# Prompt attention of a hybrid decoder step: the query blocks of each head pair taken in the order 3, 0, 2, 1, 4, 5, 6, 7

## What is computed

```python
def query_block(c):
    t0 = c * Q_BLOCK
    pos_q = t0 + jnp.arange(Q_BLOCK)
    ...
    o_c, p_c = compressed_branch(qb, pos_q, kv_cmp, slopes)
    idx, valid = select_blocks(p_c, pos_q, n_sel)
    ...
    o_s = selected_branch(qb, pos_q, kv_g, idx, valid, slopes)
    ...
    o_w = window_branch(qb, pos_q, kv_wb, pos_k, slopes)
    return gate_branches(gb, o_c, o_s, o_w)
```

## Time and profile before

| | |
|---|---|
| time, median of 3 runs | 2187.79 us (2186.11 to 2189.29) |
| profiled execution, from its first to its last instruction | 2191.0 us |
| PE (TensorE matmul) busy | 2114.1 us, 96% |
| DVE (VectorE) busy | 1035.5 us, 47% |
| ACT (ScalarE) busy | 703.1 us, 32% |
| mean granted TensorE clock | 0.984 |
| prompt attention | 169.7 to 468 us of the span |

### The profile page before, as it was taken

One profiled execution on the slowest core, in us unless ns is written; L12 is line 12 of the kernel. 1 busy time (PEld: TensorE's weight loads), 2 busy tenths in 40 slices (PEclk: granted clock), 3 DMA queues, 4 the chain that ended last, 5 costly groups with the idle time before them and its releaser, 6 DMA issues.

```text
span 2191.0 us, 33624 instructions
## 1 busy us (share of the span) xinstructions
PE 2114.1 (96%) x14200; PEld 1827.4 (83%) x14200; DVE 1035.5 (47%) x1889; ACT 703.1 (32%) x1358; POOL 162.9 (7%) x164
## 2 busy tenths in 40 slices
PE   8999999989979999999999999999999999999997
PEld 7997777758639999999888886789888998889985
DVE  2136666636442466767221225644444344444447
ACT  3226677735431344444111112121111122111222
POOL 0021000001110122221000000000000000000007
PEclk9998999999999999999999999999999999999999
DMA  9322000135573222221321204121111111111101
GB/s 225 109 71 104 11 2 11 49 124 198 180 252 108 49 61 59 57 61 42 106 58 30 58 20 135 39 86 40 49 39 50 48 48 49 39 39 58 39 20 78
DMA packets 140626, 158.91 MB, mean 73 GB/s; under 512 B 25842, under 2 KB 122315, under 8 KB 135612
## 3 DMA queue, kind: packets, MB, share of 16 engines
q1 hardware_dynamic: 132444, 113.98, 17.3%
q0 software_dynamic: 8032, 42.78, 6.3%
HBM read 141.16 MB, written 19.76 MB: 73 GB/s over the span
## 4 chain that ended last, share of the span: by engine, by line
PE 89%; DMA 3%; DVE 3%; ACT 2%; issue 1%; SPq 0%; DVEq 0%; ACTq 0%; POOLq 0%
PE PS L834 62%; PE PS L1423 5%; PE PS L1056 3%; PE PS L1036 3%; PE PS L1139 3%; DMA arena<-in_cache_sel_kv,arena 2%; PE PS L1008 2%; PE PS L1010 1%; PE PS L1124 1%; PE PS L1349 1%; PE PS L1515 1%; PE PS L1065 1%; DMA arena<-in_x_prompt 1%; PE PS L1477 1%; PE PS L1292 1%
## 5 line engine op out<-in xcount | busy, mean ns | idle before, releaser
L834 PE MATMUL PS<-x_low,w_high_mlp 128*128 128x344 f32 x1056 | 338.1, 320 | 0.0
L834 PE MATMUL PS<-w_down_high,hidden 128*128 128x512 f32 x960 | 308.2, 395 | 0.9 <-DVE w_down_low L2547 0.9
L834 PE MATMUL PS<-x_high,w_low 128*128 128x344 f32 x768 | 246.1, 320 | 0.0
L2541 DVE TENSOR_TENSOR arena<-arena,PS 128x512 f32<-128x512 f32 x244 | 167.4, 687 | 134.9 <-PE PS L834 134.7
L834 PE MATMUL PS<-x_high,w_high_mlp 128*128 128x344 f32 x720 | 230.3, 320 | 0.0
L834 PEld LDWEIGHTS PS<-w_down_high,hidden 128*128 128x128 f32 x960 | 180.1, 188 | 54.3 <-DVE arena L2541 12.0
L834 PE MATMUL PS<-w_down_low,hidden 128*128 128x512 f32 x512 | 200.9, 392 | 0.0
L834 PEld LDWEIGHTS PS<-x_low,w_high_mlp 128*128 128x128 f32 x1056 | 198.6, 188 | 2.7
L834 PE MATMUL PS<-x_low,w_high_hgrn 128*128 128x344 f32 x600 | 192.6, 321 | 0.0
L834 PE MATMUL PS<-x_high_a,w_low 128*128 128x344 f32 x480 | 154.1, 321 | 0.0
L834 PE MATMUL PS<-x_high_b,w_low 128*128 128x344 f32 x468 | 149.7, 320 | 0.0
(11 more groups left out here) (390 smaller groups left out, 4285.0 us busy)
## 6 DMA issues: line engine op xcount, KB each, us to landing
wring<-in_w_in SPq DMA_DIRECT2D x100, 256.0 KB, 3.4
wring<-in_w_up SPq DMA_DIRECT2D x64, 256.0 KB, 3.2
arena<-in_w_down SPq DMA_DIRECT2D x16, 1024.0 KB, 5.0
arena<-in_x_prompt SPq DMA_DIRECT2D x16, 512.0 KB, 3.9
x_high_kept<-x_high_att SPq DMA_DIRECT2D x1, 4128.0 KB, 14.4
arena<-in_cache_win_kv SPq DMA_DIRECT2D x8, 512.0 KB, 4.5
arena<-in_w_out SPq DMA_DIRECT2D x2, 2048.0 KB, 8.8
out<-in_cache_win_kv SPq DMA_DIRECT2D x1, 4088.0 KB
```

Of the source, the lines that this page charges most:

```text
L834: mm = pe.matmul(out, w, x, start=(start and k == 0 and i == 0), stop=(stop and k == tiles - 1 and i == 2))
L2541: dve.tensor_tensor(y, y, PS[:, 5 + d % 3, :], ALU.add).then_inc(dn_dve, 1)
```

## The change

`job` looks the query block up in a table, so that every pair takes its blocks in the order 3, 0, 2, 1, 4, 5, 6, 7. Two functions that compute i for themselves (`out` and `factors`) use the same table. The PSUM bank that collects a block's output (6 or 7) went by the parity of i and now goes by the parity of the output number, which is the same bank in the old order. The fixed places j of `stage_k`, `low_k`, `stage_q` and `slope_row` stay.

```diff
+        ORDER = (3, 0, 2, 1, 4, 5, 6, 7)
+
         def job(j):
 
-            pair, i, wc, two = j // 32, j // 4 % NQ, j // 2 % 2, j % 2
+            pair, i, wc, two = j // 32, ORDER[j // 4 % NQ], j // 2 % 2, j % 2
             return 2 * pair + two, i, wc
...
-                        mm = pe.matmul(PS[HD * two:HD * (two + 1), 6 + i % 2, c:c + P], v[0:r, :],
+                        mm = pe.matmul(PS[HD * two:HD * (two + 1), 6 + n // 2 % 2, c:c + P], v[0:r, :],
...
-                pair, i = n // NQ, n % NQ
+                pair, i = n // NQ, ORDER[n % NQ]
                 act.wait_ge(ot_ps, 2 * n + 2)
-                act.activation(aT[:, pair, P * i:P * (i + 1)], PS[:, 6 + i % 2, 3 * P:4 * P], ACT.Copy).then_inc(o_act, 1)
+                act.activation(aT[:, pair, P * i:P * (i + 1)], PS[:, 6 + n % 2, 3 * P:4 * P], ACT.Copy).then_inc(o_act, 1)
...
-                pair, i = n // NQ, n % NQ
+                pair, i = n // NQ, ORDER[n % NQ]
                 dve.wait_ge(e_act, exps(4 * n + 3))
```

## The result

| | before | changed |
|---|---|---|
| time, median of 5 runs | 2189.29 us (2186.11 to 2191.27) | 2197.77 us (2194.99 to 2200.83) |
| ratio | | 1.0036, 95% interval 1.0023 to 1.0048 |
| profiled execution, span | 2191.0 us | 2194.0 us |
| mean granted clock in it | 0.984 | 0.984 |

The new order is slower, by 0.36% in these runs. The mean of all 17 is 2193.9 us; that of the 35 executions of the kernel before beside the twelve is 2189.1. So the loss is some 4 to 5 us, 0.2%, and the first five executions lay on its high side. Executions of one kernel lie several us apart (before: 2180.37 to 2194.51), and the granted clock explains most of it, as shown further down.

A forecast was written before the change was run, and what follows sets the result against it. TensorE was taken as the bound, with waits and low clock in each pair's first four blocks. Start +0.3, waits at changes of pair -1.5 and clock there +1.9 gave +0.7: 2188.5 us, range 2181.5 to 2195.5.

The forecast's parts named there:

- The waits at the start: First pair's start: TensorE dry 1.3 us before the first turn, then 2.6 us waiting for VectorE's copy at pv(1).
- The step that failed: First pair after pv(1): half clock until 189.1 us or 3.5 us more, four blocks ending at 205.8 against 205.5, +0.3 us.
- The changes of pair: Three changes between pairs: waits shrink or move, -0.5 us each, -1.5 us in all.
- Their clock: Clock at the three changes of pair: falls last half again as long beside narrower blocks, +1.9 us in all.
- The wait of 0.45 for the second copy of job 35: Change of pair: a new wait of pv(17), block 3's last product, for VectorE's copy, 0.45 us.
- the one behind the queries: Change of pair: TensorE's wait behind ScalarE's query preparation stays, 1.4 us where it was 1.50.
- the wait for block 7's sum: Change of pair: TensorE's wait of 0.47 us for the summed output would go.
- The slower one: Rival: clock stays down beside narrow blocks, middle 2194 us, chance 0.26; test: over 7 us at half from the second pair.
- the sum of the half-clock stretches: Sign over the attention: under 10 or over 38 us at half clock, against 24.0 before, would show the prediction wrong.
- the end of the first pair's fourth block: Sign at the start: the first pair's fourth block ends at 204 to 207 us.
- The faster one: Rival: 512-wide scores opening the attention and every pair keep the clock up, -6.4 us to 2181.4, chance 0.24.

The follow-up runs named there:

- e5: The changed kernel again, unaltered, for a second profile and twelve more executions: median 2190.80 us, ratio 1.0012.
- e14: The changed kernel unaltered, profiled a third time; no execution time given.
- e3: The new block order in the first pair alone, old order in the later pairs: 2193.79 us, ratio 1.0020 to the kernel before.
- e15: The kernel before, unaltered, profiled a second time; no execution time given.
- e4: Old order in the first pair, new order in the second to fourth: 2188.75 us, ratio 0.9996 to the kernel before.
- e9: e4 with the query preparation split by head into two halves, four jobs apart, on ScalarE and VectorE: 2186.58 us, ratio 0.9986.
- e10: The kernel before (old order) with the query preparation split by head into two halves: 2184.15 us, ratio 0.9974.
- e11: The kernel before (old order) with the first score product of jobs 0 to 11 issued three times: 2186.17 us, ratio 0.9993.
- e6: The changed kernel with VectorE's key preparation moved behind job 3's second-group copy, ScalarE's left at job 2: 2193.52 us, ratio 1.0017.
- e16: The same kernel as e6, profiled a second time: 2194.28 us for that execution.
- e1: The changed kernel with the second group's key preparation moved from job 2 to jobs 22 and 26, half at each: 2193.13 us, ratio 1.0014.
- e7: The changed kernel with the first pair in order 0, 3, 2, 1, 4, 5, 6, 7: 2188.80 us, ratio 1.0000 to the kernel before.
- e8: e3 with the first score product of jobs 4 to 15 issued three times: 2187.63 us, ratio 0.9996 to the kernel before.
- e2: The kernel before (old order) with the second group's key preparation moved from job 2 to jobs 22 and 26: 2191.77 us, ratio 1.0011.
- e13: Old order in all pairs, queries split by head, first score products of jobs 0 to 11 issued three times: 2181.04 us, ratio 0.9962.

## Why the prediction was wrong

**The waits at the start were about right.** TensorE dry ahead of the first turn: 1.3 us expected, 1.58 measured. pv(1) at 184.2 to 185.0: it started at 184.74, after a wait of 2.22 for VectorE's copy (2.6 expected). Idle time up to there: 5.6 us expected, 4.0 measured.

**The step that failed is the one behind it,** "If it is at half until 189.1, 4.5 us pass 2.5 us of work, and the rest ends at 189.1 + 15.2 = 204.3; if it is at half for 3.5 us more, at 206.0. I choose 205.8". The amount of work was about right: 13.7 us at half clock and 11.6 at full one, from 184.7 to 210.0, are 13.7 / 2 + 11.6 = 18.5 us of it, where I had 17.7. The length of the half-clock stretch was not: 13.7 us after pv(1), not 4.5 to 8. Of the 4.2 us between 205.8 and 210.0 this is some 3.3 (13.7 / 2 = 6.85 us lost, where the choice left room for 3.5) and the work 0.8. (A slip beside it: 4.5 us at half clock pass 2.25 us of work, not 2.5, worth 0.2 us.) The term treats the low clock as one stretch that began at the start, as in the kernel before, and took its end, 189.1, from that kernel's single profile. In the changed kernel the clock came back at 178.7 and fell a second time at 185.5, right behind the wait at pv(1). In four profiles of this order in the first pair (the changed kernel, e5, e14 and e3) half clock took up 17.1, 17.1, 17.1 and 27.3 us of the first four blocks. That term was +0.3 and measured 40.2 - 35.8 = +4.4 between the two first profiles. From start to start, which is up to 0.3 us less than the windows shown, the first four blocks of the first pair took 39.1 to 42.1 us in those four profiles, and in five of the old order (before, e15, e4, e9, e10) 33.7 to 35.8. I had written the reason down as a rival, and priced it for the changes of pair at 3 us each but for the start at 1.5.

**Why the old order's 17 us cost less.** In the first profiles both kernels were at half clock for 17.1 us of their first pair. In the old order it lay beside blocks 0 and 1 and the keys, when TensorE would have waited for ScalarE and VectorE anyway: a slow TensorE hides such waits (idle 1.2 us). Where the clock stayed up there (e11), the waits came out, 1.16 and 0.98 us. Two profiles of before give the price, 35.8 us with 17.1 and 33.7 with 10.2 at half clock: 0.3 us per us, and e4 and e9, with 13.7 each, took 34.9 and 35.1. In the new order the waits come first, at full clock, and most of the low clock afterwards, where TensorE is the bound: there a us at half clock cost 0.4 us, by e6 and e16 (36.1 us with 6.8 and 41.6 with 20.5 at half) and by the 3.0 us for 6.8 in e5's third pair.

**Whether the wait or the narrowness is the cause** is answered in part. In every profile without added products on jobs 0 to 3 the clock fell once near the start, 171.3 to 178.2 us, behind the gaps there, which all these orders have. The second fall is the one that the changed kernel adds:

```profile
175.30:178.70 3.40, 3.40 (x21) 3.02 (x21) 1.73 (x6) 2.54 (x7) 0.00 (x0) 0.50 0.63 269
178.70:185.50 6.80, 4.34 (x51) 3.56 (x49) 5.85 (x14) 4.92 (x18) 2.02 (x2) 1.00 0.54 231
185.50:199.20 13.70, 13.70 (x73) 9.72 (x70) 4.93 (x14) 7.17 (x27) 0.00 (x0) 0.50 0.21 87
```

It was seen in all five profiles in which TensorE waited 1.45 to 2.71 us for a copy, until 184.7 to 189.1 us (the changed kernel, e5, e14, e6, e16), during the wait or at most 1.4 us behind it. It was not seen in the four with a changed first pair and no such wait (e1, e7, e3, e8), although in e1, e7 and e8 narrow blocks then ran at full clock. So the second fall goes with the wait; these are profiles set side by side, since no run took the wait away and left the keys. A loss comes without it as well: in e3 the first fall itself lasted 27.3 us.

What sets the length of a fall is open. The second one lasted 3.4, 10.2, 13.7, 13.7 and 13.7 us beside the same blocks. It did not last until a wide block came: in all five, and in e3, the clock was back before block 4's first score. In the old order it came back 0.9 to 1.3 us after block 3's first 512-wide score in four profiles (before, e4, e9, e10) and ahead of it in e15 and e2. Added products shortened the time at half clock (e8; e11 to e13 with the rival named there), so how much TensorE does seems to matter; whether it is the width, the share of the turns or something else in these blocks, no run separates. Nor is it settled how the loss divides between the waits and the clock: idle time grew by 3.5 us and busy time by 1.2 in the first profile, in e3's idle time grew by 1.1 and busy time by 5.4. They replace each other.

**The changes of pair** were forecast at -0.5 each for waits: measured -0.2 or -0.3 with the clock up (28.1 to 28.2 against 28.4), so some -0.7 in place of -1.5. Their clock was forecast at +1.9, from 1.8 us a fall; the two falls seen cost 3.0 each, but falls are rare in both orders, so about 0. That two of three pairs fell was a property of the execution that I had, not of the kernel. The wait of 0.45 for the second copy of job 35 measured 0.24 (the prediction's own two times for it, 256.95 and 256.6, give 0.35); the one behind the queries, put at 1.4, measured 1.06; the wait for block 7's sum is gone. What kept the gain small are short waits in their place: 0.42 us ahead of a turn (L1038) just before the change, and 0.36, 0.25 and 0.23 for the sums of the blocks that follow. Together, +4.4 at the start and -0.7 here make +3.7, against the 4 to 5 us of all executions; the 8.5 us between the first two medians is more than the traces show.

**The rivals and the signs.** The slower one had the right direction, but not by its own test: the second pair was at half clock for 0 us in the changed kernel, and the loss is in the first. Nor did the sum of the half-clock stretches give it away. It was to be under 10 or over 38 us if the prediction was wrong, and was 17.1 us in the changed kernel, less than the 24.0 of before: what counts is where the stretch lies. The sign that did speak is the end of the first pair's fourth block, 210.0 instead of 204 to 207. The faster one failed on its own terms: the wide scores did hold the clock at first, 0.87 in the 12.7 us ahead of pv(1) where before it was 0.50, but that is where TensorE waited.

**The Trainium skill** says in "TensorE: Matmul & The Clock Gate", Part 1, that activity releases the throttle. The runs agree with the sentence in that added products raised the mean clock, from 0.9849 to 0.9882 (e3, e8), and show that busy time in a profile is not that activity: 14.46 of 14.50 us "busy" at 0.53 in the changed kernel.

## What to carry to other kernels

Before reordering work, ask where TensorE's clock is low and what bounds the kernel there: here a low clock cost 0.3 us per us where TensorE would have waited anyway, and 0.4 where it was the bound. Waits that a slow TensorE hides come out when they fall at full clock, and behind each wait of 1.45 to 2.71 us in the first pair stood another 3.4 to 13.7 us at half clock. And when an order moves a piece that only some blocks have (here a copy by VectorE that only jobs of more than four key blocks have), look for long operations at fixed places in the same engine's program.

## What the runs showed of the hardware

- **Added matmuls made the kernel faster.** 24 redundant products in the first pair took the new order there from 2193.79 to 2187.63 us (e3, e8), and the old order's first four blocks from 34.0 or more to 33.4: with the added work, which also filled most of the 0.87 us gap, the clock did not fall at the start in any of three profiles (e11 to e13), without it it fell in each of six (before, e15, e2, e4, e9, e10).
- **The executions' spread is mostly the clock.** The mean granted clock of before's executions ran from 0.983 to 0.991. Over the twelve of e5, time against half-clock time (1 minus the mean clock, times two, times the time) has a slope of 0.41 us per us; in the other kernels of twelve executions it is 0.31 to 0.44.
- **The length of a wait does not tell how long the clock stays down.** In e11 it stayed at 1.00 through waits of 1.16 and 0.98 us; behind a wait of 2.29 us it was down for 3.4 us (e6), behind one of 2.22 for 13.7 (the changed kernel).
- The first score of the attention came at 166.7 to 173.5 us of the span in kernels that are the same up to there, so an earlier stage alone moves an execution by several us.
